# A hybrid attention, retention and convolution block: table additions one head at a time, conditioning rows copied and summed earlier

## The reference

```python
mx = jnp.split((silu_c @ ada_w[i] + ada_b[i])[:, None, :], 6, axis=-1)   # shift, scale, gate of a layer
hx = modulate_norm(xs, norm_mix[i], mx[0], mx[1])
q, k, v = jnp.split(h @ w_qkv, 3, axis=-1)
q = head_rms_norm(split_heads(q, NA_HEADS), q_gain)      # 16 heads of 64
k = head_rms_norm(split_heads(k, NA_HEADS), k_gain)
s_nb = jnp.einsum('bhqd,bhqkd->bhqk', q_r, k_nb) * NA_SCALE + bias_r
p = softmax(concatenate([s_nb, s_ctx]))
```

## Time and profile before

| | |
|---|---|
| median of 3 runs | 2592.06 us (2591.58 to 2593.57) |
| profiled execution, its own time | 2591.67 us |
| span of the profile | 2589.9 us |
| PE busy | 2467.2 us, 95% |
| DVE busy | 1827.2 us, 71% |
| ACT busy | 1020.1 us, 39% |
| POOL busy | 544.8 us, 21% |

### The profile page before, as it was taken

One profiled execution on the slowest core, in us unless ns is written; L12 is line 12 of the kernel. 1 busy time (PEld: TensorE's weight loads), 2 busy tenths in 40 slices (PEclk: granted clock), 3 DMA queues, 4 the chain that ended last, 5 costly groups with the idle time before them and its releaser, 6 DMA issues. The chain is left out here.

```text
span 2589.9 us, 36031 instructions
## 1 busy us (share of the span) xinstructions
PE 2467.2 (95%) x12660; PEld 2020.6 (78%) x12660; DVE 1827.2 (71%) x2671; ACT 1020.1 (39%) x1641; POOL 544.8 (21%) x355
## 2 busy tenths in 40 slices
PE   6997899999999999999999998999999999988999
PEld 4665488888888866788888887878888888766999
DVE  4776649888974344427888768867988877855774
ACT  2325624444231123314444226534444323345553
POOL 5103333332210020031333220003333324101000
PEclk8998999999999999999999999989999999999999
DMA  8533024545632321224445541102555555311555
GB/s 271 159 131 106 1 66 149 175 166 193 216 120 94 106 70 49 86 93 139 167 168 169 195 137 51 51 32 77 192 170 170 178 172 130 105 59 66 171 179 186
DMA packets 94887, 337.46 MB, mean 130 GB/s; under 512 B 11840, under 2 KB 13632, under 8 KB 94656
## 3 DMA queue, kind: packets, MB, share of 16 engines
q1 hardware_dynamic: 67136, 240.38, 27.4%
q10 hardware_dynamic: 24768, 86.74, 10.1%
q0 software_dynamic: 2880, 8.92, 1.6%
HBM read 334.95 MB, written 1.05 MB: 130 GB/s over the span
## 5 line engine op out<-in xcount | busy, mean ns | idle before, releaser
L616 PE MATMUL bank<-Hhi,Whi 128*128 128x512 f32 (+1 forms) x2440 | 876.8, 359 | 38.6 <-DVE Hlo L1480 15.8
L617 PE MATMUL bank<-Hlo,Whi 128*128 128x512 f32 (+1 forms) x2440 | 860.7, 353 | 0.0
L618 PE MATMUL bank<-Hhi,Wlo 128*128 128x512 f32 (+1 forms) x2440 | 860.5, 353 | 0.0
L1393 DVE TENSOR_TENSOR Wlo<-raw,Whi 128x1024 fp32r<-128x1024 f32 x424 | 639.3, 1509 | 262.1 <-ACT Whi L1059 252.8
L1059 ACT ACTIVATE Whi<-raw 128x1024 fp32r<-128x1024 f32 x424 | 448.2, 1059 | 789.4 <-DMA raw<-in_weights 727.9
L616 PEld LDWEIGHTS bank<-Hhi,Whi 128*128 128x128 f32 x2440 | 465.3, 191 | 115.9 <-issue 38.9
L617 PEld LDWEIGHTS bank<-Hlo,Whi 128*128 128x128 f32 x2440 | 465.6, 191 | 65.3 <-issue 4.6
L618 PEld LDWEIGHTS bank<-Hhi,Wlo 128*128 128x128 f32 x2440 | 465.1, 191 | 62.2
L512 POOL TENSOR_TENSOR cond_w<-cond_w,cond 128x1024 f32<-128x1024 f32 x107 | 258.2, 2413 | 643.3 <-DVE square L1417 514.8
L616 PE MATMUL bank<-Ghi,Whi 128*128 128x512 f32 (+1 forms) x770 | 268.6, 349 | 0.0
L618 PE MATMUL bank<-Ghi,Wlo 128*128 128x512 f32 (+1 forms) x770 | 266.7, 346 | 0.0
(11 more groups left out here) (226 smaller groups left out, 2942.8 us busy)
## 6 DMA issues: line engine op xcount, KB each, us to landing
raw<-in_weights SPq DMA_DIRECT2D x424, 512.0 KB, 3.3
cond_w<-in_ada ACTq DMA_DIRECT2D x160, 512.0 KB, 3.9
ada_raw<-in_ada SPq DMA_DIRECT2D x16, 512.0 KB, 15.7
ada_ring<-in_ada SPq DMA_DIRECT2D x16, 512.0 KB, 6.6
rel_in<-in_rpb POOLq DMA_DIRECT2D x48, 128.0 KB, 4.4
decay_t<-in_dist POOLq DMA_DIRECT2D x4, 640.0 KB, 4.3
X<-in_x ACTq DMA_DIRECT2D x1, 2048.0 KB, 9.8
out_y<-X SPq DMA_DIRECT2D x1, 1024.0 KB, 4.8
```

What stands on the lines that cost most here:

```text
L616: t.matmul(dst, Whi[:, st.slot, w], hi, start=start, stop=False)
L617: t.matmul(dst, Whi[:, st.slot, w], lo, start=False, stop=False)
L618: return t.matmul(dst, Wlo[:, st.slot, w], hi, start=False, stop=stop)
L1393: v.tensor_tensor(Wlo[:, st.slot, :], raw[:, st.slot, :], Whi[:, st.slot, :].bitcast(F32), ALU.subtract)\
```

## The change

On POOL the addition of a half becomes eight additions, one for each head, in a row; only the last signals `rel_ready`. On DVE, in layer 0 alone, the copy of conditioning rows for n = 0 goes from step m = 2, behind the split, to step m = 1, ahead of the split (for n = 1 to 3 it stays). The sum of the columns (`ada_store`) of each n goes from behind the `normed` of step m = 3 to ahead of it, so that both reciprocals of the last two tiles come after it.

```diff
-                    g.tensor_tensor(rel[:, some * half:some * (half + 1), :, :].rearrange("p h a k -> p (h a) k"),
-                                    rel_in[:, :, ::-1],
-                                    mask[:, None, :].to_broadcast([P, some * 6, GRID_W]), ALU.add)\
-                        .then_inc(rel_ready, 1)
+                    for q in range(some):
+                        last = g.tensor_tensor(rel[:, some * half + q, :, :], rel_in[:, 6 * q:6 * q + 6, ::-1],
+                                               mask[:, None, :].to_broadcast([P, 6, GRID_W]), ALU.add)
+                    last.then_inc(rel_ready, 1)
...
                         for m in range(4):
                             k = 8 * nth + m + 4 * i
+                            if layer == 0 and n == 0 and m == 1:
+                                ada_rows(n)
                             split(Step(p["mix"] + 8 * nth + m, 4, i))
-                            if layer == 0 and n < ADA_QK and m == 2:
+                            if layer == 0 and 0 < n < ADA_QK and m == 2:
                                 ada_rows(n)
+                            if layer == 0 and n < ADA_QK and m == 3:
+                                ada_store(ADA_START + n)
                             if m:
                                 normed(m - 1, k - 1, i, tok)
-                        if layer == 0 and n < ADA_QK:
-                            ada_store(ADA_START + n)
                         normed(3, 8 * nth + 3 + 4 * i, i, tok)
```

## The result

| | before | after |
|---|---|---|
| median (lowest to highest) | 2591.99 us (2591.58 to 2593.57) | 2569.36 us (2569.11 to 2572.02) |
| ratio, 95% interval | | 0.9907 [0.9895, 0.9920] |
| profiled execution, its own time | 2591.67 us | 2572.02 us |

What follows compares the result with a forecast made beforehand. PE is busy nearly throughout, so only its idle or low-clock stretches can give time; DVE paces layer 3's queries. 8.0 + 6.0 + 5.1 = 19.1 us off 2591.67 gives 2572.6, median forecast 2573.0; own range 2569 to 2577, stated 2569 to 2583.

Steps and rivals of the forecast that it cites:

- the start of the stage: Layer 0 near 53 us: less-stretched Hlo gives PE 0.8 to 1.3 us, counted as nothing because normed gates the next tile.
- Layer 3: Attention start in layer 3: Wlo no longer stretched, 3.3 + 3.4 - 1.6 = 5.1 us gained, bounds 3.2 and 6.4.
- part 2: Layer 0, row copy of n = 0 ahead of an earlier split: PE's hb wait goes, 8.0 us gained before 98.89.
- The assumption that carried everything: POOL's unwaiting pieces let DVE in between two; a two-input DVE instruction waits 0 to 1.0 us.
- the rival in which the pieces keep the lock: POOL's eight pieces block DVE for 8.0 us a half; gains sum to 6.7, time 2585.3 us; chance 12%.
- the consequence that I drew from the Trainium skill: GpSimd cores start the next instruction early, so pieces overlap, the port need never be free: 2585.3 instead of 2573.0.
- The price of a piece: POOL's addition of 384 elements takes 1.00 us; eight make 8.0 against 6.73 a half, and the lateness costs nothing.
- part 1: POOL's addition cut to one per head, so two-input DVE instructions wait at most one piece instead of the whole addition.
- Part 3: Layer 0, sum of columns for n = 3 moves up 4.05; lower clock goes, 1.97; together 6.0 us, or 4.0.
- The rival in which it swallows part 3: Layer 0's value projection waits for something else at its start, or slack fails: 6.0 us lost, 2579; chance 14%.
- Its slack: Middle of layer 0's value projection: DVE's wait of 7.28 us for V leaves 1.3, close but enough.
- the first term: Layer 3: the second Wlo starts earlier, putting DVE 3.2 to 4.0 us ahead, taken as 3.3.

Runs made afterwards that it cites:

- e1_again: The changed kernel once more, nothing altered: 2569.9 us, ratio 0.9901.
- e2_split: The kernel before with only the eight additions a half, both DVE moves left out: 2575.72 us, ratio 0.9929.
- e6_late_half: The kernel before, but in layer 0 POOL starts the second half's transfers only after PE has used four groups: 2593.3 us, ratio 1.0003.
- e10_evict: The changed kernel, but in layer 0's value projection ACT empties the first half's V banks one quarter earlier: 2565.36 us, ratio 0.9891.
- e11_evict_store3: The changed kernel with layer 0's V emptied one quarter earlier and the last sum of columns ahead of its split: 2563.79 us, ratio 0.9882.
- e12_split_store: The changed kernel without the early copy of conditioning rows, which stands behind its split again: 2568.37 us, ratio 0.9901.
- e8_quads: The changed kernel with POOL's additions in pieces of four heads, two a half: 2576.61 us, ratio 0.9933.
- e4_store: The kernel before with only the earlier sum of columns, n = 0 to 3: 2585.61 us, ratio 0.9961.
- e9_store3_first: The changed kernel with the last sum of columns (n = 3) also ahead of its split: 2569.7 us, ratio 0.9906.
- e3_rows: The kernel before with only the early row copy of n = 0, POOL's additions whole: 2588.82 us, ratio 0.998.

## Where the prediction held, and where it failed

The mechanism holds, the gain was forecast too small: 19.1 us against 22.6 by the medians. The step that failed in the sum is the start of the stage, counted as nothing: it gives 2.1 to 2.7 us, and they stay to the end. Layer 3 was 0.5 to 1.0 too small as well. A second step failed without changing the sum: the 8.0 us of part 2 were booked to the copy and belong to the edit of the additions.

**The lock.** The assumption that carried everything, that DVE gets in between two pieces which wait for nothing, holds. By the rival in which the pieces keep the lock, a split at the second half would have lasted until POOL was done; it lasted 1.38, and in layer 3 no split among the pieces took more than 2.07 in after and e1_again, where one took 7.01 before. The lead of 10.6 in e2_split, where that rival had 2 in part 2, is no proof of it: there the split came before the pieces. This speaks against the consequence that I drew from the Trainium skill ("GPSIMD Engine Reference", 2.1 Instruction dispatch), not against the rule itself: whether the pieces overlap on single cores isn't visible, only that the port came free between them.

**The price of a piece.** Forecast 1.00 us, measured 1.006 in the middle. The second half of layer 0 took 8.8 instead of 8.0, as one piece waited for DVE; in layer 3, with two such pieces, a half took 9.6 to 9.7. Nobody waited for POOL's additions.

**The start of the stage.** This term was mis-sized. I counted the `Hlo` stall as nothing, because the next tile would be gated by `normed` of tile 0. The lead at the third tile is 2.4 us, and it stays. The forecast of 0.8 to 1.3 for PE's gain there was itself too small. And the gate was in the wrong place: after, that `normed` ends at 76.81 (76.06 + 0.75), and PE starts tile 4 at 78.50 with no idle time ahead of it, so its own queue sets the start. In stamps of before that is 77.3, not 79.3. What could have taken the 2.4 back are the weights, and they came sooner too. ACT rounded the fifth group at 70.45, 22.2 us behind the first product; before at 72.91, 25.9 behind it:

```profile
70.45 1.06 ACT L1059 ACTIVATE Whi<-raw 128x1024 fp32r<-128x1024 f32 x1 [3.96 <-DMA raw<-in_weights]
```

Of these 3.7 us, 2.4 are PE's own lead, which frees the slot for that group sooner. The rest is a quicker landing. The prediction had allowed 0.5 us of gain for weights that come sooner. They gave none by themselves: in e2_split the group was rounded 3.8 us behind its issue, in after 6.0, and both gain the same 7.9 from 67.2 to 93.7. e6_late_half shows that the second half's transfers do hold this group up, and all the traces together that the order counts: where the transfers start at most 0.2 us ahead of the group's issue, or behind it, (e2_split, e10_evict, e11_evict_store3, e6_late_half) it is rounded 3.2 to 3.8 us behind the issue, where they start 1.5 to 7.3 us ahead of it (the other ten) 5.6 to 8.3.

**Part 2.** The step that failed is the bookkeeping. The place, the row and nearly the size are right (the lead at 93.7 is 10.3, of which 2.4 from the start; 7.9 against a forecast of 8.0), but the edit it was booked to is the wrong one. The prediction gave the copy the wait of 5.6 us that PE had behind a stretched split, while part 1 had already taken the stretch away. e2_split and e12_split_store settle it from both sides: additions without copy 10.6 and 9.4, with it 10.3 and 10.1. Two edits removed one wait, and a sum that gives each a line must ask which is enough alone. How part 1 takes the stretch away was also seen wrongly: the prediction had the split at 79.2 wait up to 1.0 between pieces, but in after, e2_split and e12_split_store it runs ahead of them. Luck has a part in that; where the pieces of four heads did meet it (e8_quads, 4.11), with the early copy, PE lost 0.7 by it. No run has the split of the copy in its old place among single pieces.

**Part 3.** 4.05 us for the move and 1.97 for the clock were forecast, 6.0 together. From 93.7 to 182.1 the lead grows by 6.0, 6.0 and 6.0 us (after, e1_again, e4_store). After 1.11 us of idle the clock didn't fall; before, after 5.15, it was granted at 0.50 from 176.80 to 180.80. What is left of the wait was the split ahead of the sum, as e9_store3_first shows.

**The value projection.** The rival in which it swallows part 3 is out: the lead is 16.3 us at 182.1 and 16.3 at 222.2, where the projection ends. PE's progress does set its middle, as assumed, but through an order: e10_evict shows 4 to 5 us more behind `V` in ACT's queue, which the prediction didn't look for, having taken the wait as given. Its slack was wrong too, without harm: it had DVE come only 8.0 us earlier, with 1.3 of the 7.28 left; DVE still waits 7.16 there.

**Layer 3.** Forecast 5.1, with bounds of 3.2 and 6.4. From 2172.1 to 2256.4 the lead grows by 6.1 in after and by 4.8 to 6.5 (mean 5.6) in the seven profiles with single pieces. The terms, on DVE and PE of after:

```profile
2169.91 1.34 DVE L1393 TENSOR_TENSOR Wlo<-raw,Whi 128x1024 fp32r<-128x1024 f32 x1 [1.56 <-ACT Whi L1059]
2171.18 3.34 DVE L1591 RECIPROCAL na_root<-na_root 128x512 f32<-128x512 f32 x1
...
2175.34 1.72 DVE L1393 TENSOR_TENSOR Wlo<-raw,Whi 128x1024 fp32r<-128x1024 f32 x1
...
2197.04 1.72 DVE L1393 TENSOR_TENSOR Wlo<-raw,Whi 128x1024 fp32r<-128x1024 f32 x1
```

```profile
PE bank L616 <- DVE Wlo L1393: 1.5, 1, 1.5
```

The stamps of after lie 15.9 lower at the layer's entry (17.1 of lead less 1.2). Before, the reciprocal behind the two splits began at 2182.48 + 8.14 = 2190.6; 2171.18 + 15.9 is 2187.1, so the first term is 3.5 (forecast 3.3). The three later waits for `Whi`, 3.4, are gone as forecast (the 1.56 above lies within the first term). The locks beyond the first term are two splits with 1.72 instead of 1.22, one in each half, 1.0 and not 1.6; in e1_again the second half stretched three (2.07, 2.02 and 1.72), and its layer 3 gives 5.0. 3.5 + 3.4 - 1.0 = 5.9, of the 6.1 seen. PE's wait for `Wlo` is 1.5, where I had said under 1.

**The whole.** Up to layer 3 the forecast was 14.0; at 182.1 it is 16.3, all of the difference being the start of the stage. Layer 3 adds 1.0 more than forecast in this execution, 0.5 in the mean of seven. 0.9 come between them in stages without an edit. Then 2.4 are lost behind the change, and 1.2 lay ahead of it, and so the profiled executions differ by 19.65 against the sum of 19.1. That these two agree is luck: 3.3 us of gain too few in the forecast's terms stand against scatter of the other sign. The median of after lies 2.7 below its own profiled execution; with that, the 0.4 by which the profiled execution of before lies below the median of 2592.06, and the 0.55 between 19.65 and 19.1, the 3.6 us between forecast and result are accounted for. What comes and goes in the stages that no edit touches is in part the granted clock, as the two windows above show; why it falls in one execution and not in the next stays open.

## What to carry to other kernels

A long elementwise instruction on POOL is a lottery for DVE's instructions with two inputs in SBUF: they lose what is left of it, and which one loses depends on a microsecond. Cut it to pieces of about the size of the DVE instructions beside it; here POOL's additions went up by 10 us in all (26.9 to 37.0) and nothing waited for them, while the kernel won 18 us from that alone by the medians, 15.4 of them at the places of the edit (e2_split). Look also at what else the pieces move: here the later second half let a split and a group of weights go first. When two edits answer the same wait, price each with the other already made. And a wait that an edit leaves as it was (here 7 us for `V`) should still be read to the instruction that is queued ahead of its releaser: that was one more edit of one line.

## What was new of the hardware

- POOL's instructions that wait for nothing still let DVE in between two of them. With single heads a DVE instruction with two inputs in SBUF took at most 0.9 us longer than alone (`Wlo` 2.07 against 1.22, e1_again), and a piece of POOL that had to wait for DVE took 1.98 instead of 1.0.
- The transfers that POOL issues slow SP's weights: with twelve of them beside it the fifth group was rounded at 72.91, and at 68.76 with them moved away (e6_late_half). Transfers issued together with the group or behind it did no such harm: 3.8 us from its issue to its rounding in e2_split, against 7.3 before, where they were issued 6.2 us ahead of it.
- After an idle time of 1.11 us (after) and of 1.74 (before, granted 1.00 from 59.50 to 65.00) PE went on at the full clock of 2.4 GHz; after 2.09 (e3_rows) it was granted 0.50, 1.2 GHz, from 60.50 to 63.90, and after 5.64 (before) 0.51 from 84.60 to 88.90. The length of the idle time alone doesn't tell: 2.13 us in e3_rows (to 87.99) and 3.55 in e2_split were followed by the full clock, 3.56 before by the half.
